# Linear-attention values: two heads at a time, in units of 512 rows and 512 columns

## The reference

```python
GLA_HEADS, GLA_HEAD_K, GLA_HEAD_V, CHUNK = 4, 128, 256, 64

proj = h @ w_in[l]                      # h: 512 x 1024
q, k, v, r, lr_f, lr_b, u, g_a, g_b = jnp.split(proj, split_points, axis=-1)
...
o_fwd = gla_chunked(qh, kh, vh, af, include_diag=True)
o_bwd = jnp.flip(gla_chunked(jnp.flip(qh, 2), ..., include_diag=False), 2)
o = o_fwd + o_bwd
o = o * lax.rsqrt(jnp.mean(o * o, axis=-1, keepdims=True) + EPS)
o = o * gla_norm * silu(r)
y_a = o @ w_branch_gla[l]
merged = jax.nn.sigmoid(g_a) * y_a + jax.nn.sigmoid(g_b) * y_b
```

## Time and profile before

| what | us |
|---|---|
| runs | 1327.5, 1328.1, 1328.2 |
| median of the runs | 1328.1 |
| span of the profiled execution, first to last instruction | 1326.3 |
| TensorE busy in it | 1315.1 (99%) |
| VectorE / ScalarE / GpSimd busy in it | 722.0 / 576.6 / 338.3 |

### The profile page before, as it was taken

How to read it: one execution, slowest core, us unless ns; L and a number is a source line. 1 busy time by engine, 2 the same in 40 slices (tenths; PEclk the granted TensorE clock), 3 DMA queues, 4 the chain that set the end, 5 groups by cost and what they waited for, 6 DMA issues and landing times.

```text
span 1326.3 us, 21060 instructions
## 1 busy us (share of the span) xinstructions
PE 1315.1 (99%) x8153; PEld 1092.6 (82%) x8153; DVE 722.0 (54%) x1293; ACT 576.6 (43%) x797; POOL 338.3 (26%) x95
## 2 busy tenths in 40 slices
PE   8999999999999999999999999999999999999997
PEld 6888989888888888888888888777788888888886
DVE  4643241664556666666744480222397778845336
ACT  5744363462344322222223252555665565654333
POOL 6421222225333000000134404422211112124441
PEclk9999999999999999999999999999999999999999
DMA  6332322224234455545433343333223222323321
GB/s 188 97 95 64 95 63 82 77 80 159 95 96 131 142 140 140 141 139 140 127 108 89 106 106 110 95 100 90 63 65 88 73 65 66 95 65 101 121 96 64
DMA packets 199637, 134.55 MB, mean 101 GB/s; under 512 B 5719, under 2 KB 190920, under 8 KB 199574
## 3 DMA queue, kind: packets, MB, share of 16 engines
q1 hardware_dynamic: 198342, 131.41, 34.1%
q10 hardware_dynamic: 848, 1.60, 0.4%
q0 software_dynamic: 384, 0.64, 0.2%
HBM read 131.51 MB, written 2.12 MB: 101 GB/s over the span
## 4 chain that ended last, share of the span: by engine, by line
PE 98%; DVE 1%; ACT 0%; DMA 0%; issue 0%; ACTq 0%; DVEq 0%
PE acc L496 22%; PE acc L498 22%; PE acc L497 22%; PE acc L505 3%; PE acc L507 3%; PE acc L506 3%; PE acc L520 1%; PE acc L519 1%; PE acc L521 1%; PE acc L2645 1%; PE acc L2644 1%; PE acc L2643 1%; PE acc L2498 1%; PE acc L2500 1%; PE acc L2499 1%; PE mid L2543 1%
## 5 line engine op out<-in xcount | busy, mean ns | idle before, releaser
L474 POOL TENSOR_TENSOR wlo<-raw,whi 128x2048 fp32r<-128x2048 f32 (+1 forms) x74 | 323.3, 4369 | 948.9 <-ACT whi L470 948.8
L496 PE MATMUL acc<-hhi,whi 128*128 128x512 f32 x896 | 353.4, 394 | 0.0
L497 PE MATMUL acc<-hlo,whi 128*128 128x512 f32 x896 | 349.0, 390 | 0.0
L498 PE MATMUL acc<-hhi,wlo 128*128 128x512 f32 x896 | 348.9, 389 | 0.0
L470 ACT ACTIVATE whi<-raw 128x2048 fp32r<-128x2048 f32 (+1 forms) x108 | 199.9, 1851 | 106.8 <-PE acc L498 90.3
L498 PEld LDWEIGHTS acc<-hhi,wlo 128*128 128x128 f32 x896 | 168.2, 188 | 35.6
L496 PEld LDWEIGHTS acc<-hhi,whi 128*128 128x128 f32 x896 | 168.3, 188 | 34.4 <-issue 0.9
L497 PEld LDWEIGHTS acc<-hlo,whi 128*128 128x128 f32 x896 | 168.4, 188 | 33.7 <-issue 0.2
L1290 DVE TENSOR_TENSOR wlo<-raw,whi 128x2048 fp32r<-128x2048 f32 (+1 forms) x34 | 76.5, 2249 | 22.8 <-ACT whi L470 22.8
L505 PE MATMUL acc<-hhi,whi 128*128 128x512 f32 x160 | 65.4, 409 | 0.0
L496 PE MATMUL acc<-ahi,whi 128*128 128x512 f32 x165 | 64.4, 390 | 0.0
(11 more groups left out here) (421 smaller groups left out, 2306.4 us busy)
## 6 DMA issues: line engine op xcount, KB each, us to landing
raw<-in_w_in_dram SPq DMA_DIRECT2D x56, 512.0 KB
raw<-in_w_in_dram SPq DMA_DIRECT2D x26, 1024.0 KB
raw<-in_w_ffn_in_dram SPq DMA_DIRECT2D x44, 512.0 KB
ada<-in_w_ada_dram SPq DMA_DIRECT2D x24, 512.0 KB, 3.9
raw<-in_w_ffn_out_dram SPq DMA_DIRECT2D x16, 704.0 KB
raw<-in_w_out_dram SPq DMA_DIRECT2D x8, 1024.0 KB
xnat<-in_x_dram SPq DMA_DIRECT2D x8, 512.0 KB, 6.1
raw<-in_w_branch_gla_dram SPq DMA_DIRECT2D x4, 1024.0 KB
```

Of the source, the lines that this page charges most:

```text
L474: nc.gpsimd.tensor_tensor(wlo[:, slot, 0:n], raw[:, slot, 0:n], whi[:, slot, 0:n].bitcast(f32), ALU.subtract).then_inc(s_unit_lo, 1)
L496: nc.tensor.matmul(acc[bank][:, :], h, xh[:, k, :], start=(k == 0), stop=False)
L497: nc.tensor.matmul(acc[bank][:, :], h, xl[:, k, :], start=False, stop=False)
L498: last = nc.tensor.matmul(acc[bank][:, :], lo, xh[:, k, :], start=False, stop=(k == nk - 1))
```

## The change

The 16 units of the four heads stay 16, but their borders move. `HEAD_U` gives the first unit of each head: 1, 6, 9, 14 (and 17 for the next stage). Heads 0 and 2 have five units, q and k, ga, two of values, r; heads 1 and 3 have three, q and k, ga, r. A value unit holds 512 of the 1024 rows and 512 columns, the values of two heads. PE goes through both of them with four tiles open, one for each 128 tokens in a bank of its own: first half of the contraction into all four, then the second half. `gv` becomes twice as large (two heads) and moves to another place in SBUF, where the pooling weights come later; so SP waits for the last head's outputs (`s_go`) before it loads `pwraw`. The head loops of PE, ACT, DVE and SP are written out. In heads 1 and 3 PE does the state products between the two ga tiles and the outputs behind the second one. ACT splits the r unit of heads 0 and 2 when PE has signalled the end of the first value half (`s_out_half`).

Beside that, key blocks that nobody reads are no longer transposed: three blocks of four for each direction in the linear attention, three of four in HGRN, with the copies and two of DVE's multiplies narrowed to match.

```diff
+HEAD_U = (1, 6, 9, 14, 17)
+def value_unit(h):
+    return HEAD_U[h // 2 * 2] + 2
+def gate_unit(h):
+    return HEAD_U[h + 1] - 1
...
-    gv = at("gv", A0 + 36, [P, TT, DV])
+    gv = at("gv", A0 + 98, [P, 2, TT, DV])
...
+                load(u + 1, head_slot(u + 1), kview(w_in, C_GA + h * 256, 256))
+                if h % 2 == 0:
+                    for a in range(2):
+                        v = value_unit(h) + a
+                        load(v, head_slot(v), kview(w_in[a * L:(a + 1) * L, :], C_V + h * DV, 2 * DV), nk=KT // 2,
+                             ncol=2 * DV)
+                load(gate_unit(h), head_slot(gate_unit(h)), kview(w_in, C_R + h * DV, 256))
...
+            sp.wait_ge(s_go, 2 * GLA_HEADS)
             sp.dma_start(pwraw.rearrange("p (g n) -> p g n", g=NG), inp["w_pool_group"][0].rearrange("g p n -> p g n"))\
...
             def head_evict_v(h):
-                for c in range(2):
-                    b, full, _ = TL(U_HEAD, 4 + c, 8, h)
+                for t in range(TT):
+                    b, full, _ = TL(value_unit(h), t)
                     act.wait_ge(s_acc_full, full)
-                    act.wait_ge(s_bias_out, 16)
-                    A(gv[:, 2 * c:2 * c + 2, :].rearrange("p t v -> p (t v)"), acc[b][:, :], ACT.Copy)\
+                    A(gv[:, :, t, :], acc[b][:, :].rearrange("p (h v) -> p h v", v=DV), ACT.Copy)\
                         .then_inc(s_acc_free[b], 1)
...
-                    A(kdT[:, d, :, :].rearrange("p t k -> p (t k)"), M[d][:, :], ACT.Copy).then_inc(s_kdT, 1)
+                    A(kdT[:, d, d:TT - 1 + d, :].rearrange("p t k -> p (t k)"), M[d][:, d * P:(TT - 1 + d) * P], ACT.Copy)\
+                        .then_inc(s_kdT, 1)
...
+            def gate_split(h):
+                u = gate_unit(h)
+                if h % 2 == 0:
+                    act.wait_ge(s_out_half, h // 2 + 1)
+                    split_hi(act, u, head_slot(u), lin=0)
+                else:
+                    head_split(u)
 
             head_evict_ga(0)
+            act.wait_ge(s_bias_out, 16)
+            gate_split(0)
             head_evict_v(0)
-            head_split(0, 3)
+            head_split(HEAD_U[1])
             head_evict_r(0)
             derive(0)
-            with act.Fori(1, GLA_HEADS) as h:
+            for h in range(1, GLA_HEADS):
                 g = h - 1
-                head_split(h, 0)
+                head_split(HEAD_U[h] + 1)
                 head_evict_qk(h)
                 gla_kdT(g)
...
+                if h % 2 == 0:
+                    head_split(value_unit(h))
+                    head_evict_ga(h)
+                    head_split(value_unit(h) + 1)
+                    gate_split(h)
+                    gla_squares(g)
+                    gla_sum_hi(g)
+                    head_evict_v(h)
+                else:
+                    gate_split(h)
+                    head_evict_ga(h)
+                if h % 2:
+                    head_split(HEAD_U[h + 1])
+                    gla_squares(g)
+                    gla_sum_hi(g)
+                else:
+                    head_split(HEAD_U[h + 1])
                 gla_rs(g)
                 head_evict_r(h)
                 derive(h)
...
+            def head_values(h, a):
+                u = value_unit(h) + a
+                pe.wait_ge(s_unit_lo, u + 1)
+                for t in range(TT):
+                    b, _, free = TL(value_unit(h), t)
+                    if a == 0:
+                        pe.wait_ge(s_acc_free[b], free)
+                    ts = slice(t * P, (t + 1) * P)
+                    for k in range(KT // 2):
+                        kk, ws = a * (KT // 2) + k, slice(k * L, (k + 1) * L)
+                        h_, l_ = whi[:, head_slot(u), ws], wlo[:, head_slot(u), ws]
+                        mm(acc[b][:, :], hhi[:, kk, ts], h_, start=(kk == 0), stop=False)
+                        mm(acc[b][:, :], hhi[:, kk, ts], l_, start=False, stop=False)
+                        last = mm(acc[b][:, :], hlo[:, kk, ts], h_, start=False, stop=(kk == KT - 1))
+                    if a == 1:
+                        last.then_inc(s_acc_full, 1)
+                if a == 0:
+                    last.then_inc(s_out_half, 1)
...
+                pe.wait_ge(s_unit_lo, u + 2)
+                head_tile(u + 1, 0)
+                if h == 0:
                     decay(4)
                     decay(5)
+                elif h % 2:
+                    gla_kv(g)
+                head_tile(u + 1, 1)
+                if h == 0:
                     decay(6)
                     decay(7)
+                elif h % 2:
+                    gla_out(g)
+                else:
                     gla_kv(g)
+                if h % 2 == 0:
+                    head_values(h, 0)
+                    if h > 0:
+                        gla_out(g)
+                    head_values(h, 1)
+                pe.wait_ge(s_unit_lo, gate_unit(h) + 1)
+                head_tile(gate_unit(h), 0)
+                if h > 0:
+                    gla_sum(g)
+                head_tile(gate_unit(h), 1)
...
-                for t in range(TT):
+                for t in range(d, TT - 1 + d):
                     last = nc.tensor.transpose(M[d][:, t * P:(t + 1) * P], kf[:, d, t * P:(t + 1) * P], ident[:, :])
...
             def hg_transposes(g):
                 pe.wait_ge(s_h_op, g * 2 + 1)
-                for t in range(TT):
+                for t in range(TT - 1):
                     last = nc.tensor.transpose(M[1][:, t * P:(t + 1) * P], hkd[:, t * P:(t + 1) * P], ident[:, :])
```

More of the change, by code:

```diff
@@ L481, in unit_count, with head_slot @@
             return (u - slot) * 16
[L483 to L485 removed]
+        def head_slot(u):
+            return (u + 1) % 2
         def raw_free(sp, u):
@@ L510, in pe_part @@
                 last.then_inc(s_acc_full, 1)
[L512 to L522, removed]
         def kview(w, c0, n):
@@ L585, in _ @@
             sp.dma_start(lr_sum[:, :], inp["strip_sum"]).then_inc(s_lr_in, 16)
-            def head_loads(h, u):
-                load_pair(u, 0, w_in, C_Q + h * DK, C_K + h * DK)
-                if isinstance(u, int):
+            for h in range(GLA_HEADS):
+                u = HEAD_U[h]
+                load_pair(u, head_slot(u), w_in, C_Q + h * DK, C_K + h * DK)
+                if h == 0:
                     sp.wait_ge(s_pool_prep, 3)
@@ L1477, in gla_final @@
                 for j in range(2):
-                    b, _, free = TL(U_HEAD, 6 + j, 8, g)
+                    b, _, free = TL(gate_unit(g), j)
                     dve.wait_ge(s_gt, g * 2 + j + 1)
@@ L1485, in _ @@
             gla_derive(0)
-            with dve.Fori(1, GLA_HEADS) as h:
+            for h in range(1, GLA_HEADS):
                 gla_mask(h - 1)
@@ L1994, in _ @@
             nc.gpsimd.tensor_copy(masks[:, :, :], mask_src[:, :, :]).then_inc(s_masks, 1)
[L1995 to L2001, removed]
+            for u in range(3, U_POOL):
+                if u in [HEAD_U[h + 1] + 1 for h in range(GLA_HEADS)]:
+                    pool.wait_ge(s_unit_lo, u + 1)
+                else:
+                    split_lo(pool, u, head_slot(u))
             pool.wait_ge(s_unit_hi, U_POOL + 1)
@@ L2132, in _, with head_tile @@
                 .then_inc(s_bias_mm, 1)
-            def head_tiles(h, c, j):
-                tile(U_HEAD, c, c // 2 % 2, j, 8, h)
+            def head_tile(u, j):
+                tile(u, j, head_slot(u), j)
             def decay(i):
@@ L2196, in gla_kv @@
                         t = n if d == 0 else TT - 1 - n
-                        last = mm(state_bank(d, n), kdT[:, d, t, :], gv[:, t, :], start=True, stop=True,
+                        last = mm(state_bank(d, n), kdT[:, d, t, :], gv[:, g % 2, t, :], start=True, stop=True,
                                   skip_group_check=True)
@@ L2202, in gla_kv @@
                     t = 2 - d
-                    last = mm(state_bank(d, 2), kdT[:, d, t, :], gv[:, t, :], start=True, stop=True,
+                    last = mm(state_bank(d, 2), kdT[:, d, t, :], gv[:, g % 2, t, :], start=True, stop=True,
                               skip_group_check=True)
@@ L2225, in gla_sum @@
                 mm(M[2][:, :], mean_dv[:, :], exl[:, :], start=False, stop=True).then_inc(s_gsum, 1)
[L2227 to L2233, removed]
-                g = h - 1
-                if gla:
-                    pe.wait_ge(s_unit_lo, h * 4 + U_HEAD + 1)
-                    head_tiles(h, 0, 0)
-                    head_tiles(h, 1, 1)
-                    gla_scores(g)
-                pe.wait_ge(s_unit_lo, h * 4 + U_HEAD + 2)
-                if gla:
-                    b, _, free = TL(U_HEAD, 2, 8, h)
-                    pe.wait_ge(s_acc_free[b], free)
-                    pe_part(b, 1, 0, 0, KT)
-                else:
-                    head_tiles(h, 2, 0)
+            def head_values(h, a):
+                u = value_unit(h) + a
+                pe.wait_ge(s_unit_lo, u + 1)
+                for t in range(TT):
```

(28 more changed lines are left out.)

73 lines of the change are left out of this document (26 added, 47 removed).

## The result

The changed kernel takes 1331.27 us (median of 9 runs, 1330.55 to 1332.5), the kernel before 1327.91 in the same comparison; the ratio is 1.0026, 95% interval 1.0018 to 1.0034. It is slower by 3.4 us, which is what the sum of the prediction gave (1331.5). Two of its terms are losses, a stall of PE and a slow clock behind it, so the experiments ask above all whether those two are what they were taken for.

What follows compares the result with a forecast made beforehand. TensorE (PE) was taken to bound the kernel, busy 1315.1 of 1326.3 us. The terms -2.5 - 1.7 + 5.6 + 2.0 = +3.4 us, added to the median of 1328.1, gave 1331.5 us, range 1329.0 to 1334.0.

Steps and rivals of the forecast that it cites:

- Values: Value matmuls on PE: 192 of 512 columns replace 384 narrow ones, 43.5 us instead of 46.0, a gain of 2.5 us.
- Transposes: Key transposes on PE: two fewer in each of 4 heads, one in each of 8, a gain of 1.7 us.
- Banks of the first value stage: First value unit: PE waits for bank 3 from 52.4 to 58.0 us, until ACT's first sigmoid; a loss of 5.6 us.
- Clock: Behind the PE stall: the clock falls and PE runs 4 us at half speed, a loss of 2.0 us (0 to 2.5).
- Splits: Splits on ACT and GpSimd, 6.3 us together, are covered by 10.9 us of PE's second value half; price 0.
- order in the odd heads: State products and outputs stand between gate-branch tiles on PE, each covered by 5.44 us where they had 11; price 0.
- SP: Pooling-weight load moves behind the last head's output products: 33 us of cover against a delay of some 5; price 0.
- loops: Head loops written out: PE showed no wait at their ends, so price 0.
- No stall: Rival: bank 3 is free when PE asks in the first value stage, only gains are left, 1323.9 us; chance 0.14.
- The clock holds: Rival: PE stalls in the first value stage but the clock does not fall, 1329.5 us; chance 0.12.
- A second wait: Rival: PE's gate-branch input or a split comes 1 us late in each of three heads, 1334.5 us; chance 0.14.
- narrow matmuls cost no more than half a wide one: Rival on the value matmuls: the 2.5 us gain goes, time 1334.0 us; no separate chance, put in the upper end.

Runs made afterwards that it cites:

- e6: Changed kernel with first-head gate-branch banks copied out early by ACT and all key transposes, copies and multiplies put back; 1325.72 us, ratio 0.9983 to the kernel before.
- e2: Kernel before with only the unread key blocks no longer transposed, copies and multiplies narrowed; 1326.34 us, ratio 0.9987.
- e10: Changed kernel with 23 identity matmuls on PE before its wait for the third value tile, run beside e9 and e11; 1329.73 us, ratio 1.0012.
- e11: Changed kernel with the first head's two gate-branch banks copied out early by ACT, sigmoids later in place, run beside e9 and e10; 1323.77 us, ratio 0.9967.
- e9: Changed kernel unaltered, run again on the same chip as e10 and e11; 1332.03 us, ratio 1.0031 to the kernel before.
- e5: Changed kernel with 23 identity matmuls into an idle bank on PE before its wait for the third value tile; 1330.30 us, ratio 1.0017 to the kernel before.
- e4: Kernel before with only its head loops written out on SP, ACT, DVE, GpSimd and PE; 1328.22 us, ratio 1.0002.
- e1: Changed kernel with ACT copying the first head's two gate-branch banks out inside its decay loop, sigmoids later in place; 1323.53 us, ratio 0.9967 to the kernel before.
- e7: Changed kernel with the first head's two sigmoids moved ahead of ACT's wait for DVE's lbt; 1327.89 us, ratio 0.9997 to the kernel before.
- e3: Changed kernel with 46 identity matmuls into an idle bank on PE before its wait for the third value tile; 1333.95 us, ratio 1.0045 to the kernel before.

## Why the prediction was right, point by point

- *Values, -2.5 us.* e6 has -2.4 in both measures. Right, and the 0.5 us that followed from the spacing given in the Trainium skill, page "TensorE: Matmul & The Clock Gate", section "Back-to-back issue gap", is ruled out by e6's interval (at least 0.8 parts in a thousand, 1.1 us).
- *Transposes, -1.7 us.* e2 has -1.5. By the traces two transposes of a linear-attention head are worth 0.85 - 0.63 = 0.22 us and one of an HGRN head 0.52 - 0.42 = 0.10, together 4 x 0.22 + 8 x 0.10 = 1.7. Right within the measurement.
- *Banks of the first value stage, +5.6 us.* The trace has the wait at the tile and on the engine named, 5.4 us as the view of waits counts it, and 58.29 - 52.70 = 5.6 from when the next matmul could have started. Between e10 and e11 it is 5.5 to 6.0. Right.
- *Clock, +2.0 us (0 to 2.5).* The trace has it fall during the stall and stay low for 4.6 us of work, 2.2 us lost by the spacings; e9 against e10 gives 2.3. By the single traces it is 2.5 (changed kernel against e5) and 2.0 (e9 against e10), by the medians of the first pair, on two chips, 1.0. The mechanism was right, and 2.0 lies inside what was measured. One reading behind it is less sure than it was put. That the clock was low in the first 5 us was taken from the doubled spacing; the granted clock of that time reads 1.00, as the line below shows (third figure from its end), so the record does not bear it out, and what doubled the spacing there stays open. The upper end of 5 us at half speed rested on it; the 4.6 us of work measured at 0.50 are close to that.

```profile
4.00:8.00 4.00, 4.00 (x22) 4.00 (x21) 1.43 (x3) 1.87 (x6) 0.00 (x0) 1.00 1.02 408
```

- *The four terms together.* -2.4 - 1.5 + 5.5 + 2.5 = +4.1 in the matmul stretch of the traces, where +3.4 was forecast; the medians say +3.4 and, on another chip, +3.7. The last two terms are differences between kernels of the same table, so that the four add up shows little more than that the gains of e2 and e6 do. That the forecast and the first of these medians agree to 0.1 us is luck in part: the clock alone differs by more than that from run to run, and four microseconds at half speed were a choice between 0 and 5.
- *Splits, order in the odd heads, SP, loops: 0.* PE has no wait in the later heads, and e4 shows the loops alone. The room in front of the second to third head's gate branch grew from 0.6 to 1.1 us. In e2, with the narrower multiplies and the two transposes less but the old order, it is 0.9 (136.3 to 137.3); the rest was not tried by itself. The load of the pooling weights goes out at 274.3 us, where it was 264.4, lands 3.9 us later, and its reader on ACT runs at 302.5, where it was 297.5: against its reader it is late by 4.9 us, the "some 5" of the prediction, and 24 us of cover are left.
- *The rivals.* "No stall" is what e1 makes of the kernel, and it gives the time that this rival had, 1323.9. "The clock holds" is what e5 and e10 make of it, with 1329.5 forecast and 1330.3 and 1329.7 measured. "A second wait" did not come. That narrow matmuls cost no more than half a wide one is refuted by e6.

What the change set out to do works. It is undone by one wait that it brings along: value units with four open tiles ask for two banks that ACT, held up by its wait for DVE's lbt and a table load, has not emptied; the first of them comes free 5.6 us after PE asks for it.

## What to carry to other kernels

When the number of banks that a stage holds open grows, go through the tiles that sat in the added banks and look up when they are really emptied, not when they were finished; a late evictor that nobody waited for becomes the bound. Where the engine that empties has a long chain in front, a plain copy out of the bank and the function later, in place, frees it for about 0.6 us of that engine (0.58 and 0.57 in e1). And a stall of TensorE can have a second price behind it, the slow clock: 1.0 to 2.5 us here behind stalls of 5.4 us, and in some runs behind one of 2.1. It is to be counted in before a stall is accepted.

## What the runs showed of the hardware that was not expected

- A short idle stretch can be enough: in the trace of e7 PE stood 2.1 us, and right behind that the granted clock was 0.50 for 3.3 us of work, where 1.03 us at the start of the run had left the spacing alone. By the times of the other runs of e7 it was not so in each of them.
- At the lower clock a wide matmul takes 0.427 us (0.227 at the upper), a narrow one 0.213 (0.120): both less than a doubling. The Trainium skill, page "TensorE: Matmul & The Clock Gate", section "Back-to-back issue gap", gives the cold spacing as columns over 1.2 GHz, by which one estimates 0.427 and 0.213 us, and the trace agrees. It is the warm spacing that is longer here than that section of the Trainium skill has it.
- The price of the slow clock differs from run to run. In the nine runs of the changed kernel the mean granted clock is 0.998 in the four fastest (1330.55 to 1330.82 us) and 0.996 or 0.997 in the other five (1331.27 to 1332.50); e7, above, spreads over 2.9 us. Kernels whose clock holds spread over 1.0 to 1.5 us (e1, e2, e5, e6, e10, e11), so not all of a spread is the clock's. A single trace can put the term at 2.0 or at 2.5.
- A matmul of plain float32 operands, 128 by 128, leaves two records and takes 0.22 us at a granted clock of 1.00 (e3: 46 in 10.2 us), twice a transpose of the same size, which leaves one (six in 0.63 us, 0.105 each).
